# The prompt's top-128 selection: sixteen rounds of "eight largest, then strike them out" in place of a 31-bit threshold search

## The reference, cut to what matters

```
s = einsum('bqhd,bld->bqhl', qi, ki) * IDX_DIM ** -0.5
score = einsum('bqhl,bqh->bql', relu(s), wi)
score = where(causal, score, NEG_INF)
_, idx = lax.top_k(score, topk)          # topk = min(256, 512 // 4) = 128
...
logits = where(valid, einsum(q, k[idx]) * HEAD_DIM ** -0.5, NEG_INF)
out = softmax(logits) @ v[idx]
```

## Time and profile before

| what | value |
|---|---|
| median of three runs | 1100.62 us (1098.14 to 1101.87) |
| profiled execution, its own time | 1100.96 us |
| its span, first to last instruction | 1099.2 us |
| mean granted TensorE clock over the span | 0.970 |

### The profile page before, as it was taken

One profiled execution on the slowest core, in us unless ns is written; L12 is line 12 of the kernel. 1 busy time (PEld: TensorE's weight loads), 2 busy tenths in 40 slices (PEclk: granted clock), 3 DMA queues, 4 the chain that ended last, 5 costly groups with the idle time before them and its releaser, 6 DMA issues.

```text
span 1099.2 us, 18944 instructions
## 1 busy us (share of the span) xinstructions
PE 1008.2 (92%) x6442; PEld 517.3 (47%) x6442; DVE 628.7 (57%) x2011; ACT 289.8 (26%) x614; POOL 171.2 (16%) x292
## 2 busy tenths in 40 slices
PE   6999999899789899898999999999988998989994
PEld 3345444345544455554453644443455444645541
DVE  4337996577974343541651599855979634444233
ACT  3221111431121433232322211144112144323131
POOL 8631001010400000001825010001013000000000
PEclk9999999999989999899999999999998998989998
DMA  8642776357875646265643358635678656536611
GB/s 272 169 138 81 248 268 192 116 196 240 314 240 174 244 130 222 84 237 199 191 126 87 97 197 272 225 115 197 192 263 303 209 189 234 172 114 217 198 51 57
DMA packets 106513, 205.29 MB, mean 187 GB/s; under 512 B 15495, under 2 KB 23894, under 8 KB 106418
## 3 DMA queue, kind: packets, MB, share of 16 engines
q1 hardware_dynamic: 87250, 150.25, 40.9%
q0 software_dynamic: 19168, 53.84, 15.6%
HBM read 194.00 MB, written 10.14 MB: 186 GB/s over the span
## 4 chain that ended last, share of the span: by engine, by line
PE 67%; DVE 13%; DMA 8%; SPq 4%; issue 3%; ACT 2%; POOL 0%; DVEq 0%; ACTq 0%; POOLq 0%
PE bank L1517 29%; PE bank L1806 10%; PE bank L1491 5%; DVE r L1046 5%; DMA pg<-in_cache_k_dram 5%; SPq L677 4%; PE bank L1698 4%; PE bank L1634 4%; DMA pg<-in_cache_v_dram 3%; PE bank L1597 2%; PE bank L1613 2%; PE bank L1764 2%; PE bank L1775 2%; PE bank L1842 1%; PE bank L1868 1%
## 5 line engine op out<-in xcount | busy, mean ns | idle before, releaser
L1517 PE MATMUL bank<-wr,ht 128*128 128x512 f32 (+1 forms) x1024 | 440.6, 579 | 4.0 <-ACT sh L935 2.8
L1517 PEld LDWEIGHTS bank<-wr,ht 128*128 128x128 f32 x1024 | 189.5, 193 | 209.7 <-issue 199.3
L1046 DVE TENSOR_SCALAR_CACHE_REDUCE r<-r,sel_i 128x1088 bf16<-128x1088 f32 (+3 forms) x248 | 187.4, 793 | 3.6
L715 POOL DMA_DIRECT2D wr<-in_w_in_dram x64 | 45.7, 719 | 354.1 <-PE bank L1517 293.7
L1491 PE MATMUL bank<-wr,ht 128*64 128x256 f32 (+1 forms) x640 | 76.1, 396 | 5.5 <-ACT gr L860 4.1
L1698 PE MATMUL bank<-pg,rs 128*32 128x256 f32 x1024 | 70.2, 416 | 11.5 <-DMA pg<-in_cache_v_dram 7.7
L1634 PE MATMUL bank<-pg,r 128*32 128x256 f32 x1024 | 64.7, 383 | 15.5 <-DMA pg<-in_cache_k_dram 15.4
L631 POOL DMA_DIRECT2D pg<-in_cache_kidx_dram x128 | 68.5, 539 | 46.6 <-issue 41.5
L1491 PEld LDWEIGHTS bank<-wr,ht 128*64 128x64 f32 x640 | 47.4, 146 | 32.4 <-issue 12.8
L715 POOL DMA_DIRECT2D wr<-in_w_out_dram x16 | 11.3, 710 | 321.9 <-PE bank L1806 139.8
L1806 PE MATMUL bank<-wr,gr 128*128 128x512 f32 x128 | 58.5, 600 | 2.7 <-DVE ht L1428 2.7
(11 more groups left out here) (264 smaller groups left out, 1240.7 us busy)
## 6 DMA issues: line engine op xcount, KB each, us to landing
pg<-in_cache_k_dram SPq DMA_DIRECT2D x256, 256.0 KB, 4.4
pg<-in_cache_v_dram SPq DMA_DIRECT2D x256, 256.0 KB, 4.4
wr<-in_w_in_dram POOLq DMA_DIRECT2D x56, 512.0 KB, 4.9
wr<-in_w_out_dram POOLq DMA_DIRECT2D x16, 512.0 KB, 4.9
r<-in_x_prompt_dram SPq DMA_DIRECT2D x8, 512.0 KB, 7.1
pg<-in_cache_kidx_dram POOLq DMA_DIRECT2D x128, 32.0 KB, 2.3
pg<-in_cache_kidx_dram SPq DMA_DIRECT2D x128, 32.0 KB, 2.4
wr<-in_w_in_dram POOLq DMA_DIRECT2D x8, 256.0 KB, 3.5
```

The lines of the kernel that those rows point to most:

```text
L715: pool.dma_start(W[n % 2][:, n4 * 2:n4 * 2 + 2, 0:w], src[:, n4 * 2:n4 * 2 + 2, :])\
L1046: ins = nc.vector.tensor_scalar(junk[i][0:m, 0:part.shape[1]], part, sc, None, ALU.is_ge, ALU.add, accum_out=CNT[0:m, i:i + 1])
L1517: mm = pe.matmul(b[0:m, 0:w], HT[:, k, rt * P:rt * P + m], weights[k], start=(k == 0), stop=(k == KC - 1), skip_group_check=(k1 - k0 < KC))
```

## The change

The prompt's search is replaced. One round takes, of each of the three parts, the eight largest scores of every row (`max`, into `BEST`), and then overwrites those eight in the part by -3e38 (`match_replace`). Sixteen rounds strike out 128 scores. What is struck out is what is kept: `pmask` writes 0 where the part holds -3e38 and -1e30 elsewhere. The sign step, the 31 bits, and the three `take` steps are gone. The sample's search stays as it was. The multiplication by the first head's weight gets "+ 0.0" as a second operation in the same instruction.

```diff
+TAKEN = -3e38
+ROUNDS = KP // 8
...
-    s += [("turn", 0, 1), ("exp", 1), ("psel", 0, 3)]
+    s += [("turn", 0, 1), ("exp", 1), ("psel", 0, 2)]
...
-    s += [("turn", 0, 2), ("psel", 3, 6)]
+    s += [("turn", 0, 2), ("psel", 2, 4)]
...
-    s += [("V", 0, 2), ("turn", 0, 3), ("psel", 6, 10)]
+    s += [("V", 0, 2), ("turn", 0, 3), ("psel", 4, 6)]
...
-    s += [("V", 0, 3), ("turn", 0, 4), ("psel", 10, 12)]
+    s += [("V", 0, 3), ("turn", 0, 4), ("psel", 6, 7)]
...
-    s += [("K", 2, 1), ("V", 0, 4), ("turn", 1, 0), ("od", 0), ("psel", 12, 15)]
+    s += [("K", 2, 1), ("V", 0, 4), ("turn", 1, 0), ("od", 0), ("psel", 7, 9)]
...
-    s += [("V", 1, 0), ("turn", 1, 1), ("psel", 15, 18)]
+    s += [("V", 1, 0), ("turn", 1, 1), ("psel", 9, 11)]
...
-    s += [("K", 2, 2), ("psel", 18, 21)]
+    s += [("K", 2, 2), ("psel", 11, 13)]
...
-    s.append(("psel", 21, 24))
+    s.append(("psel", 13, 15))
...
-        0: (... ("psel", 24, 27)], []),
-        1: (... ("z", "uv", 0), ("psel", 27, BITS)]),
-        2: (... ("z", "uv", 1), ("ptake", 0), ("ptake", 1)]),
-        3: (... ("z", "uv", 2), ("ptake", 2)]),
+        0: (... ("psel", 15, ROUNDS)], []),
+        1: (... ("z", "uv", 0), ("pmask",)]),
+        2: (... ("z", "uv", 1)]),
+        3: (... ("z", "uv", 2)]),
...
+        BEST = SP_[0][:, P:P + 24].rearrange("p (i n) -> p i n", i=3)
...
+            def take_best(first, end, parts):
+                for _ in range(first, end):
+                    for i, part in enumerate(parts):
+                        ins = nc.vector.max(BEST[:, i, :], part)
+                    then(ins)
+                    for i, part in enumerate(parts):
+                        ins = nc.vector.match_replace(part, BEST[:, i, :], part, TAKEN)
+                    then(ins)
...
-                            nc.vector.tensor_scalar(SCP[:, c0:c0 + w], r[:, 0:w], wcol, None, ALU.mult)
+                            nc.vector.tensor_scalar(SCP[:, c0:c0 + w], r[:, 0:w], wcol, 0.0, ALU.mult, ALU.add)
...
+                    elif s[0] == "pmask":
+                        for part in parts:
+                            ins = nc.vector.tensor_scalar(part, part, TAKEN, -BIG, ALU.not_equal, ALU.mult)
+                        then(ins)
```

More of the change, by code:

```diff
@@ L312, in _order @@
     turned("kT", 3)
-    s.append(("psel", 21, 24))
+    s.append(("psel", 13, 15))
     filler = {
-        0: ([("z", "gc", 3), ("V", 1, 1), ("turn", 1, 2), ("psel", 24, 27)], []),
-        1: ([("z", "uv", ST)], [("zk", "uv", 0, 0, 4), ("K", 2, 3), ("z", "uv", 0), ("psel", 27, BITS)]),
[2 rows of a table removed]
+        0: ([("z", "gc", 3), ("V", 1, 1), ("turn", 1, 2), ("psel", 15, ROUNDS)], []),
+        1: ([("z", "uv", ST)], [("zk", "uv", 0, 0, 4), ("K", 2, 3), ("z", "uv", 0), ("pmask",)]),
[2 rows of a table added]
         4: ([("zk", "uv", 3, 0, 4), ("V", 1, 4)], [("mask", 2, 0), ("K", 3, 0), ("z", "uv", 3), ("mask", 2, 1), ("od", 1), ("mask", 2, 2), ("exp", 2)]),
@@ L457, in build @@
         SP_ = [r1[:, 3264 + 512 * i:3264 + 512 * (i + 1)] for i in range(3)] + [r1[:, 2208:2720]]
-        PJUNK = [SP_[i][:, P:P + 256].bitcast(mybir.dt.bfloat16) for i in range(3)]
+        BEST = SP_[0][:, P:P + 24].rearrange("p (i n) -> p i n", i=3)
         MXP, NB_ = r1[:, 4848:4880], r1[:, 4880:4912]
@@ L1108, in sample_take @@
                 nc.vector.tensor_tensor(SCR, SC, SCR, ALU.add).then_inc(selm_ready, 1)
[L1110 to L1125, removed]
             def mask_and_max(l, p, part_no):
@@ L1369, in _ @@
                         if h == 0:
-                            nc.vector.tensor_scalar(SCP[:, c0:c0 + w], r[:, 0:w], wcol, None, ALU.mult).then_inc(rs_dve, 1)
+                            nc.vector.tensor_scalar(SCP[:, c0:c0 + w], r[:, 0:w], wcol, 0.0, ALU.mult, ALU.add).then_inc(rs_dve, 1)
                         else:
@@ L1381, in _ @@
                     elif s[0] == "psel":
[L1382 to L1390, removed]
+                        take_best(s[1], s[2], parts)
+                    elif s[0] == "pmask":
+                        for part in parts:
+                            ins = nc.vector.tensor_scalar(part, part, TAKEN, -BIG, ALU.not_equal, ALU.mult)
+                        then(ins)
                     elif s[0] == "od":
```

## The result

| | before | changed |
|---|---|---|
| median | 1100.48 us (1098.14 to 1101.87, 4 runs) | 1089.58 us (1086.97 to 1092.02, 4 runs) |
| ratio | | 0.9909, 95% interval 0.9887 to 0.9931 |
| profiled execution, its time / span | 1100.96 / 1099.2 us | 1092.02 / 1090.3 us |

A forecast was written before the change was run, and what follows sets the result against it. PE was taken to bound the kernel, DVE counting only where PE waits for it. From 1100.96 us, +1.4 (rounds against bits), -0.7 (`za` wait) and -1.3 (ranking) gave 1100.4 us; range 1095 to 1110.

The forecast's parts named there:

- +1.4 - 0.7 - 1.3: Both layers: rounds against bits from `od 0` to first logits +1.4 us, `za` wait -0.7, layer 0 ranking -1.3; sum -0.6.
- I take 3.45: One DVE round over three parts, two instructions each, lasts 3.45 us; eight replace twelve bits of 26.9 us per layer.
- The lower working, 3.38: DVE round of 3.38 us if each `match_replace`'s small companion overlaps; 3.6 us if it does not.
- slope: DVE from `od 0` to first logits: each us of round length moves the kernel's time by 16 us.
- The break-even at 3.36: DVE from `od 0` to first logits: round time beyond 3.36 us is handed to PE in full, twice.
- DVE issues no DMA and none is moved: Transfers: only copies and logits queue behind DVE's later rounds, page loads follow PE; key-page waits costed as unchanged.
- Rival C: PE's waits for DVE become waits for pages; gain and loss swallowed, 1101 us. Shares chance 0.47 with the forecast, 1098 to 1104.
- I count nothing there: Ranking ahead of heads 6 and 7: removal saves 1.3 us in layer 0, nothing in layer 1, whose wait is 0.8 us.
- rival B: Selection leaves PE's path with a round of 3.1 us or less, shorter waits may spare half clock: 1096 or less; chance 0.21.
- `za` gone: PE's 0.3 us wait before the second tile disappears in each layer, counted as -0.7 us in all.
- T: Length of one DVE selection round, forecast at 3.45 us, between bounds of 2.4 and 5.7 us.
- The lower bound of 2.4 us: DVE round of 2.4 us if both new instructions ran at TENSOR_SCALAR's rate, 476 ns where TENSOR_TENSOR needs 692.

The follow-up runs named there:

- e7_pad59: Changed kernel with an idle 384-column DVE instruction behind each of the eight rounds from `od 0` to the first logits (round 3.81 us): 1.0009 of the kernel before.
- e4_before_shift: Kernel before, same 31 bits, two moved ahead of `od 0`, leaving ten instead of twelve up to the first logits: 0.9982 of the kernel before.
- e6_rounds_early: Changed kernel with three rounds moved ahead of `od 0`, leaving five up to the first logits: 0.9960 of the kernel before.
- e2_take_time: Changed kernel with idle DVE work where the ranking stood, 7.7 us ahead of heads 6 and 7, 5.3 us ahead of 8 and 9: 0.9999 of the kernel before.
- e5_same_time: Changed kernel with idle DVE instructions so each place of the rounds and ranking lasts as long as before: 1.0014 of the kernel before.
- e9_rank_time_67: Changed kernel with 7.7 us of idle DVE work ahead of the logits of heads 6 and 7 alone: 0.9989 of the kernel before.

## Why the prediction was wrong

The prediction named the right two places, but its sum nearly cancelled (+1.4 - 0.7 - 1.3), so that small errors decided. Two of its terms were mis-sized (the round and the ranking), the clock was left at nothing, and one statement on the transfers was false. The first three made the gain too small, the last by itself would have made it too large.

- *The round, "I take 3.45".* It is 3.21 us. The lower working, 3.38 with overlapping loads, was nearer, and even that added up 0.17 us too much. The three `max` last 1.47 us where I had 1.54, and each `match_replace` is 14 to 17 ns shorter than TENSOR_TENSOR. By the sum's own slope of 16 us for each us, the term on the path turns from +1.4 to -2.4 us and the forecast becomes 1096.6 us. I had argued for the middle of two workings although the row of the count's companion, at 83 ns, spoke for the lower; the loads take 85 ns.
- *The slope.* The break-even at 3.36 was a sound reading of the two chains, and `e7_pad59` has the slope above it: 3.2 us a layer for 3.2 us of DVE. Below it the slope holds about in layer 1 and not in layer 0. The table has 0.5 to 1.9 us less at the front in both layers together, not 2.4. The step that failed is "DVE issues no DMA and none is moved", with "PE waits for those alone" behind it: POOL's store of the keys waits for DVE's `rope k`, the weight chunk stands behind that store, and value pages, which the sum has nowhere, come to limit PE. In `e4_before_shift` they take the whole of what DVE gives up (waits of 5.6 and 6.1 us where there was none). Rival C was real for this one place.
- *The ranking, "I count nothing there".* I counted 1.3 us in layer 0 and nothing in layer 1, because PE's wait on `sh` read 0.8 us there. In that execution PE had just waited 1.4 us for value pages, so that DVE had caught up. The row was in the view of layer 1 (760 to 880 us) and not in the earlier trace rows:

```profile
PE bank L1698 <- DMA pg<-in_cache_v_dram: 1.4, 1, 1.4
```

  Every other kernel with DVE busy there has 24.4 us or more in both layers, every one without 23.1 to 23.8, except one layer of `e6_rounds_early` and of `e7_pad59` with waits for pages. It is 2 x 1.3 us: 1095.3 us.
- *The clock.* The sum has it at nothing; I gave it to rival B as a chance. At the sample tile of `uv` alone the changed kernel is 2.2 to 3.7 us shorter over both layers (6.5 and 5.3 us before, 3.6 to 5.2 after), about as much as the ranking gives, though some of the half clock only moved ahead into the front. Over all runs 1 to 5 us go with the clock. That it follows the waits is what the runs suggest: the slow eight instructions stand behind four of the seven waits on `sh` of 1.8 us and more, in `e2_take_time` (both layers), `e4_before_shift` and `e5_same_time`, and behind none of the 21 shorter ones. What sets one off in one execution and not in the next stays open.

With the round and the ranking put right the sum is 1095.3 of 1100.96 us, a ratio of 0.9949, and two of the three comparisons have it inside their interval. That is luck in part: the sum so mended takes too much from the front and nothing from the clock, and these two errors pull opposite ways. The first comparison's 0.9909 has it outside: what is left, about 4 us, is the clock and chance, which the repeated comparisons, 0.9939 and 0.9956, do not separate further.

What was right: DVE's work (56 us less forecast, 57 measured), `za` gone, the rest idle DVE, and nothing to win ahead of heads 8 and 9. Rival B was the likeliest reading of the result, and its chance of 0.21 was too low: it wanted T at 3.1 or less, and the time got there with 3.21, by the ranking and the clock besides. The Trainium skill's rule that a match and replace is two instructions (VectorE: DVE Perf Modes, "Two Vector instructions with no wait between them") is borne out by the MATCH_VALUE_LOAD rows; the sum had allowed for it. The lower bound of 2.4 us did not come either: neither new instruction runs at TENSOR_SCALAR's rate (676 and 675 ns for 512 columns, not 476). Two numbers of the rivals do not follow from the prediction's own formula: T = 5.7 gives 1136 us, not 1138, and 1096 us is reached at T = 3.18 already, not at 3.1.

## What to carry to other kernels

Where two chains race and each is worth more than twenty microseconds, a tenth of a microsecond in the repeated step decides: work it out from the rows at their own precision, and do not round towards caution. A stage that is the same in every layer should cost the same in every layer; if the wait reads smaller in one, look for another wait just ahead of it that hid it, before counting nothing. And a wait removed by re-ordering is only a gain if the transfers behind it are in. Ask which queues wait for the engine that you speed up, even if it issues no transfer itself: here POOL's stores waited for DVE, and a weight chunk stood behind them. Moving two steps and looking at PE's waits is a cheap test before a rewrite is judged.

## What the runs showed of the hardware

- MAX8 over 256, 384 and 512 fp32 columns takes 423, 542 and 676 ns (0.99 ns for each column from 256 to 512), MATCH_REPLACE8 409, 543 and 675 ns (1.04 ns) with 85 ns of MATCH_VALUE_LOAD ahead. In all sixteen rounds of both layers each instruction stays within 9 ns of these times. Selecting 128 of each row in three parts takes 51.4 us of DVE's time (sixteen rounds of 3.21), against 69.4 for 31 bits.
- PE's waits of 1.8 to 2.0 us on one and the same step were followed by a stretch at 1.2 GHz four times (eight instructions in 5.3 to 5.4 us for 3.70, in three profiled executions) and by full clock three times: the kernel before (1.99 us), layer 1 of `e5_same_time` (1.99 us) and `e9_rank_time_67` (2.00 us). Waits of 0.7 to 1.2 us on this step were followed by full clock all 21 times.
- With the DMA engines full (share 1.02 over 16 us), the last value pages reached PE 3.4 us later, counted from the same PE step, when a weight chunk of four times 512 KB was issued 2.2 us earlier (`e4_before_shift` against the kernel before, layer 0). Whether the one caused the other was not tested.
